# A hybrid decoder layer on one core: the prologue's input second in the queue, two modulation products in high and low halves, and two projection tiles begun between them

## What is computed

```python
def mixer_layer(x, c, ...):
    mod = jax.nn.silu(c) @ w_ada + b_ada          # 1024 -> 3072
    shift, scale, gate = jnp.split(mod, 3, axis=-1)
    h = rms_norm(x, pre_norm_w) * (1.0 + scale[:, None]) + shift[:, None]
    proj = h @ w_in                               # 1024 -> 3080, then pooling and gated delta rule
    ...
    y = jnp.concatenate([y_a, y_b], axis=-1) @ w_out
    x = x + gate[:, None] * rms_norm(y, post_norm_w)
```

## Time and profile before

| | before |
|---|---|
| median of 3 runs | 1133.2 us (1130.15 to 1133.69) |
| the profiled execution | 1131.2 us, its span 1129.4 us |
| TensorE busy | 1097.0 us, 97% |
| VectorE, ScalarE, GpSimd busy | 654.2, 358.0, 225.2 us |

### The profile page before, as it was taken

The page is one execution under the profiler, slowest core; times in us unless marked ns, Lnnn a source line. Parts: engine busy times, 40 slices in busy tenths (PEclk is TensorE's granted clock), DMA queues, the critical chain, the costliest instruction groups (busy, mean ns, idle before and its releaser), DMA issues.

```text
span 1129.4 us, 16484 instructions
## 1 busy us (share of the span) xinstructions
PE 1097.0 (97%) x6120; PEld 880.2 (78%) x6120; DVE 654.2 (58%) x1344; ACT 358.0 (32%) x713; POOL 225.2 (20%) x226
## 2 busy tenths in 40 slices
PE   7999999989999999999999999999999999999995
PEld 1578567877878888887878888887878888888774
DVE  1579884656345784555266883654346863454634
ACT  2365331234524511133324511224325420111201
POOL 1333443553400011231000002230000010522000
PEclk9999998999999999999999999999999999999998
DMA  9597555433756553224555552225673342322354
GB/s 367 199 321 269 207 199 194 151 129 132 269 209 244 200 187 123 102 76 156 219 205 205 192 191 100 108 80 186 224 275 114 148 149 76 113 75 75 110 203 164
DMA packets 44963, 196.09 MB, mean 174 GB/s; under 512 B 8858, under 2 KB 9626, under 8 KB 27348
## 3 DMA queue, kind: packets, MB, share of 16 engines
q1 hardware_dynamic: 44884, 195.03, 47.3%
HBM read 150.20 MB, written 44.81 MB: 173 GB/s over the span
## 4 chain that ended last, share of the span: by engine, by line
PE 68%; DVE 1%; issue 1%; POOL 0%; DVEq 0%; ACT 0%; POOLq 0%
PE acc L1991 12%; PE acc L1993 11%; PE acc L1992 11%; PE ring L2033 11%; PE acc L2020 2%; PE ring L2020 2%; PE ring L2022 2%; PE ring L2021 2%; PE acc L2022 2%; PE acc L2021 2%; PE ring L2178 2%; PE ring L2040 1%; PE ring L2049 1%; PE ring L2050 1%; PE ring L2209 1%
## 5 line engine op out<-in xcount | busy, mean ns | idle before, releaser
L1991 PE MATMUL acc<-hhi,wsl 128*128 128x512 f32 x768 | 315.8, 411 | 1.1 <-DVE y L1300 1.1
L1993 PE MATMUL acc<-hhi,wsl 128*128 128x512 f32 x768 | 301.2, 392 | 0.0
L1992 PE MATMUL acc<-hlo,wsl 128*128 128x512 f32 x768 | 300.4, 391 | 0.0
L1991 PEld LDWEIGHTS acc<-hhi,wsl 128*128 128x128 f32 x768 | 145.2, 189 | 32.7 <-issue 5.1
L1993 PEld LDWEIGHTS acc<-hhi,wsl 128*128 128x128 f32 x768 | 144.7, 188 | 32.0
L1992 PEld LDWEIGHTS acc<-hlo,wsl 128*128 128x128 f32 x768 | 145.3, 189 | 27.0 <-issue 1.4
L1187 DVE SCALAR_TENSOR_TENSOR cacc<-raw,cw,cacc 128x512 f32<-128x512 f32 x144 | 113.7, 789 | 5.1
L1777 POOL TENSOR_TENSOR wsl<-wraw,wsl 128x512 fp32r<-128x512 f32 x64 | 87.8, 1389 | 141.1 <-ACT wsl L871 141.1
L900 ACT ACTIVATE raw<-acc 128x512 f32<-128x512 f32 x48 | 28.6, 597 | 161.6 <-PE acc L1993 161.5
L1095 DVE TENSOR_TENSOR hlo<-htmp,hhi 128x512 fp32r<-128x512 f32 x32 | 22.1, 692 | 62.2 <-ACT hhi L845 61.9
L2020 PE MATMUL acc<-wsl,yhi 128*128 128x512 f32 x128 | 53.0, 414 | 1.8 <-DVE y L1300 1.6
(11 more groups left out here) (298 smaller groups left out, 1873.0 us busy)
## 6 DMA issues: line engine op xcount, KB each, us to landing
wsl<-kept_w SPq DMA_DIRECT2D x96, 1024.0 KB, 4.8
kept_w<-wsl SPq DMA_DIRECT2D x32, 1024.0 KB, 6.2
wraw<-in_w SPq DMA_DIRECT2D x64, 256.0 KB, 3.5
wada<-in_w_ada SPq DMA_DIRECT2D x8, 1024.0 KB, 13.0
xb<-in_x SPq DMA_DIRECT2D x16, 512.0 KB, 6.3
xres<-in_x SPq DMA_DIRECT2D x16, 512.0 KB, 5.7
out_y<-ytok SPq DMA_DIRECT2D x16, 512.0 KB, 8.2
wada<-in_w_ada SPq DMA_DIRECT2D x16, 256.0 KB, 4.8
```

What stands on the lines that cost most here:

```text
L1991: nc.tensor.matmul(acc[t % 2][:], w[:, 0, k], hi[:, k], start=(k == 0), stop=False)
L1992: nc.tensor.matmul(acc[t % 2][:], w[:, 0, k], lo[:, k], start=False, stop=False)
L1993: last = nc.tensor.matmul(acc[t % 2][:], w[:, 1, k], hi[:, k], start=False, stop=(k == KT - 1))
```

## The change

SyncE's queue now has the input directly after product 0 and the small tables, then product 1, the sample rows, the three raw halves, product 2, product 3.

Products 2 and 3 are no longer float32 matmuls. ScalarE copies each half of `wada[j]` (128 x 2048) to `wadh` in float32r, VectorE subtracts in place to `wadl`; `cin2` holds the high and the low half of the 9 rows side by side, 18 in all. `modulate_halves` runs two one-pass matmuls per k-step, with high and low weights, into a bank of `spare`. The turned result of 18 rows is folded to 9 columns by a matmul with `fold`. Products 0 and 1 remain.

The prologue's `h` is made as in the later blocks (`front_h`): ScalarE writes `htmp` and, in a second activation, `hhi`; VectorE only subtracts. ScalarE takes three raw halves ahead of the first `h` and the fourth behind the cuts.

```diff
+            def modulation_hi(j, e):
+                ks = slice(e * KT // 2, (e + 1) * KT // 2)
+                act.wait_ge(ada_in[j][e], 16)
+                nc.scalar.activation(wadh[j - 2][:, ks], wada[j][:, ks], ACT.Copy).then_inc(s_whi, 1)
+
+            for n in range(3):
+                half_hi(n)
+            act.wait_ge(s_half, 3)
+            front_h(act, PROLOGUE, 0)
+            front_h(act, PROLOGUE, 1)
+            modulation_hi(2, 0)
+            front_h(act, PROLOGUE, 2)
+            front_h(act, PROLOGUE, 3)
+            modulation_hi(2, 1)
+            modulation_hi(3, 0)
+            modulation_hi(3, 1)
+            half_hi(3)
+            act.wait_ge(s_half, 6)
+            for m in range(4, 8):
+                front_h(act, PROLOGUE, m)
...
+            def modulation_lo(j, e):
+                ks = slice(e * KT // 2, (e + 1) * KT // 2)
+                dve.wait_ge(s_whi, 2 * (j - 2) + e + 1)
+                nc.vector.tensor_tensor(wadl[j - 2][:, ks], wada[j][:, ks], wadh[j - 2][:, ks].bitcast(F32), ALU.subtract
+                                        ).then_inc(s_wlo, 1)
...
+            def modulate_halves(j, e):
+                pe.wait_ge(s_wlo, 2 * (j - 2) + e + 1)
+                if j == 2 and e == 0:
+                    pe.wait_ge(s_cin2, 3)
+                if j == 3 and e == 0:
+                    pe.wait_ge(s_half, 2)
+                rows = spare[4 - 2 * (j - 1)][0:2 + 2 * NS, :]
+                for k in range(e * KT // 2, (e + 1) * KT // 2):
+                    nc.tensor.matmul(rows, cin2[:, k], wadh[j - 2][:, k], start=(k == 0), stop=False)
+                    last = nc.tensor.matmul(rows, cin2[:, k], wadl[j - 2][:, k], start=False, stop=(k == KT - 1))
+                if e:
+                    last.then_inc(s_mod, 1)
...
             def first_tiles():
-                for t in range(2):
-                    for k in range(4):
-                        tile(0, t, k)
-                front_pe(pe, PROLOGUE, 7)
-                for t in range(2):
-                    for k in range(4, KT):
-                        tile(0, t, k)
+                for k in range(2):
+                    tile(0, 0, k)
+                    tile(0, 1, k)
+                front_pe(pe, PROLOGUE, 3)
+                modulate_halves(2, 0)
+                for k in range(2, 4):
+                    tile(0, 0, k)
+                    tile(0, 1, k)
+                modulate_halves(2, 1)
+                modulate_halves(3, 0)
+                front_pe(pe, PROLOGUE, 4)
+                front_pe(pe, PROLOGUE, 5)
+                front_pe(pe, PROLOGUE, 6)
+                turn_rows(2)
+                modulate_halves(3, 1)
+                turn_rows(3)
+                for k in range(4, KT):
+                    tile(0, 0, k)
+                    tile(0, 1, k)
+                    if k == 4:
+                        front_pe(pe, PROLOGUE, 7)
```

More of the change, by code:

```diff
@@ L682, in _ @@
                 sp.dma_start(xb[:, i], a["x"][0][:, i]).then_inc(x_in.sem, 16)
-            modulation(2)
+            modulation(1)
             sp.dma_start(xrow, a["xs"]).then_inc(sm_x0, 16)
@@ L723, in _ @@
                 raw_half(n)
+            modulation(2)
             modulation(3)
@@ L1131, in _ @@
                                                op0=ALU.add, op1=ALU.mult).then_inc(s_half, 1)
[L1132 to L1137 removed]
+            row_copy(0)
+            front_xn(dve, PROLOGUE)
+            row_copy(1)
+            dve.wait_ge(s_prm, 32)
+            modulation_columns(0)
+            front_lo(dve, PROLOGUE, 0)
+            front_lo(dve, PROLOGUE, 1)
+            modulation_lo(2, 0)
+            front_lo(dve, PROLOGUE, 2)
+            front_lo(dve, PROLOGUE, 3)
+            modulation_lo(2, 1)
+            modulation_lo(3, 0)
+            row_copy(2)
+            modulation_lo(3, 1)
+            row_copy(3)
+            modulation_columns(1)
+            for m in range(4, 8):
+                front_lo(dve, PROLOGUE, m)
             dve.wait_ge(*done("pool", "rx"))
@@ L1922, in turn_rows @@
                 for i in range(4):
-                    last = nc.tensor.transpose(spare[j // 2][:, 36 * (j % 2) + 9 * i:36 * (j % 2) + 9 * (i + 1)],
-                                               rows9[j][:, i * P:(i + 1) * P], ident[0:1 + NS, 0:1 + NS])
+                    col = 36 * (j % 2) + 9 * i
+                    to, part = spare[j // 2][:, col:col + 9], rows9[j][:, i * P:(i + 1) * P]
+                    if j < 2:
+                        last = nc.tensor.transpose(to, part, ident[0:1 + NS, 0:1 + NS])
+                    else:
+                        last = nc.tensor.matmul(to, part, fold[:], start=True, stop=True)
                 last.then_inc(s_tr, 1)
```

81 lines of the change are left out of this document (30 added, 51 removed).

## The result

| | kernel before | changed kernel |
|---|---|---|
| median of the runs | 1132.6 us (4 runs) | 1144.6 us (4 runs, 1142.1 to 1145.6) |
| ratio to before | | 1.0107 [1.0086, 1.0128] |
| profiled execution, time (span) | 1131.2 (1129.4) | 1142.1 (1140.3) |
| landmark: end of the two first tiles | 55.0 | 64.9 |
| small gate matmuls start | 60.7 | 73.5 |

The change costs 12.0 us by the medians and 10.9 by the two spans. I forecast slower, by 5, with 1141 as the upper end: the sign held, the size did not.

A forecast was written before the change was run, and what follows sets the result against it. TensorE, busy 97%, was taken as the bound, so only the prologue's end counted: +9.1 us to the second factors, −4.1 to the landmark, +5.0 in sum. Forecast 1137.2 us, range 1132.5 to 1141.

The forecast's parts named there:

- Steps 1 and 2: Input loading and product 1: squares from 14.4 us, 5.0 earlier; TensorE waits for weights to 16.9, finishes at 24.1.
- Step 3: VectorE's normalising: held by GpSimd's subtractions, three in a row adding 1.25 us; input ready at 27.4 us, before 31.2.
- rival A: Normalising on VectorE: GpSimd does not hold it, input ready at 23.7 us, only +1.6 us, 1133.8; chance 0.15.
- Steps 4 and 5: Chain to the modulation factors: first at 30.4 us, second at 51.6 (42.5 before), paced by ScalarE's cuts and VectorE's subtractions.
- First factors: Modulation columns' first half, after transposes and row turns: ready at 30.4 us, against 31.6 before.
- Second factors: Modulation columns' second half, after cuts, subtractions and quarter products: ready at 51.6 us, 9.1 later than before.
- Step 6: Second factors to the landmark: 8.4 us against 12.5 before, landmark at 60.0.
- Rival B: TensorE drops to its lower clock in the prologue's new gaps: +7 us, 1139.2; chance 0.13.
- gap of 1.54 us: TensorE's wait in before, filled by transposes behind it: read as losing nothing to the lower clock.
- late next: SyncE's queue behind the last input transposes: near 56 us, 6.5 later; raw halves still covered, else 1 us or so.

The follow-up runs named there:

- x6: Changed kernel with GpSimd's first three subtractions held until VectorE has normalised all four input pieces: 1140.2 us, ratio 1.0083.
- x4: Changed kernel with its queue and TensorE order, but products 2 and 3 in float32 as before, without cuts: 1150.4 us, ratio 1.0160.
- x1: Changed kernel plus three filler matmuls in each of three long TensorE waits in the prologue: 1144.8 us, ratio 1.0118.
- x9: Kernel before plus four dummy VectorE additions ahead of the gates' row copy, first pass only, lengthening one TensorE wait: 1136.4 us, ratio 1.0032.
- x13: Kernel before with x9's dummy additions and 18 filler matmuls in the wait they lengthen: 1132.3 us, ratio 1.0004.
- x2: Changed kernel with x1's fillers and 14 more behind the gate projection: 1143.3 us, ratio 1.0092.
- x18: Changed kernel with x1's fillers, VectorE's gates copy ahead of the first convolution, and 3 fillers behind the gates' matmuls: 1136.1 us, ratio 1.0047.
- x14: Kernel before plus five filler matmuls in its 1.2 us wait ahead of the gates' small matmuls, first pass only: 1130.5 us, ratio 0.9980.
- x15: x10 with VectorE's gates copy ahead of the first convolution, first pass only, and 3 fillers instead of 14 behind the gates' matmuls: 1129.0 us, ratio 0.9976.
- x10: Changed kernel with its prologue reordered (early cuts, GpSimd's subtractions behind the normalising), plus 4 and 14 fillers in two long waits: 1131.0 us, ratio 0.9989.
- x12: Changed kernel with before's input queue order, product 1 ahead of the input and product 2 behind it: 1151.8 us, ratio 1.0162.
- x3: Kernel before with only the loads in the new order; TensorE's order and float32 products stay: 1134.0 us, ratio 1.0017.
- x16: Kernel before with VectorE's gates copy ahead of the first convolution, first pass only: 1130.9 us, ratio 0.9988.

## Why the prediction was wrong, step by step

**Steps 1 and 2** held nearly: squares from 15.15 us (14.4), product 1 waits to 17.65 and ends at 24.7 (24.1). The input came 0.7 us later than I read from the megabytes ahead of it.

**Step 3** held: four normalising instructions in 6.70 us, ready at 28.1 (27.4), and x6 showed that it is GpSimd's hold, as step 3 had it against rival A. The Trainium skill ("SBUF — State Buffer", "Who interferes with whom") has whichever engine comes first hold the shared ports for a whole instruction, while the other is blocked. The trace agrees that VectorE is blocked, and goes beyond it in length: the 3.96 us here cover three instructions of GpSimd back to back.

**Steps 4 and 5**, the prices: cuts 1.9 and subtractions 2.25 us were right (1.92, and 4.49 for two); the last subtraction, beside GpSimd's, took 2.78. First factors 31.0 (30.4). Second factors 54.9 (51.6). The terms that I sized wrongly are two. The *turns with the fold* I had at 0.41 each, as before's turns; they are not transposes but float32 matmuls against a matrix, and take 1.05, so 2 × 0.64 = 1.3 us more (in x4, which turns with transposes, the second one takes 0.41). And the third group of transposes came 2.3 us late, 1.7 of it the clock (x1: 36.0), so ScalarE waited.

**Step 6**: second factors to landmark 10.0 us (8.4). In x1, at full clock, it is 8.45. This step was right but for the clock.

**Rival B** is what happened, and I gave it 0.13. I priced it at 2 us above the forecast. The profile shows 3.2 at the landmark (64.9 against 61.7), and then a third stretch that I did not name, of a further 1.6 us. The mistake was in the reading of before: I took its gap of 1.54 us without harm as the rule for gaps twice as long, and its first 169 us without a half-clock stretch as a property of the kernel rather than of a TensorE that was hardly ever without matmuls. And I wrote that every wait behind the prologue was about a microsecond. The view of TensorE's waits in before has one of 4.6 us, for VectorE (us in total, times, longest):

```profile
PE ring L2033 <- DVE wb L1610: 4.6, 1, 4.6
```

It ends at 252.1 us. The granted clock is 1.00 at 248 to 250 us, 0.89 at 250 to 252, 0.50 from 252 to 258 and 0.90 at 258 to 260: 6.8 us at half clock, begun in the wait. The price of a long wait stood in before's own trace. I had counted four waits of 2.5 to 3.3 us myself; x9 and x13 now show what one such wait brings. The rule of the Trainium skill that I cited there ("TensorE: Matmul & The Clock Gate", part 4, PE-mode transpose: transposes do not count as work for the gate) pointed the right way, but no run here parts transposes from plain waiting, so it is neither shown nor refuted.

**"So the change is worth exactly the microseconds by which it moves the end of the prologue"** was the failed assumption, and no rival had it growing: everything behind the landmark was to move as a block. Behind it the late second half let GpSimd's subtractions fall on VectorE's operations, and the gates' copy, third in that row, came 2.0 us later (+6.8 to +8.75 in x2). x18 moves the copy and the 2 us are gone. In the changed kernel's own profile this stretch lost 2.9 us, the three slowed operations on 512 columns included. Of what I listed as late next, SyncE's queue waited 27.8 us where before's waited 9.0, to 60.9 (I had 56); the tiles' weights showed no wait of TensorE.

The sum as it now stands, in the terms of the prediction: 5.0 forecast, + 0.6 first factors, + 1.3 turns (together +6.8 measured), + 2.0 gates' copy (8.75), + about 3 for the clock = 12. The last is the rest of the medians (12.0 − 8.75 = 3.3), not measured by itself, and not a sum over stretches (x2's total, with all four waits filled, is still 10.4 us above before by its ratio, 6.7 to 14.2). How many such stretches there are differs from run to run (mean clock 0.982 to 0.989 in the four of the changed kernel). The one near 170 us, behind waits that the change does not touch, is in the profiles of before, x14 and x15 and not in those of the changed kernel, x10 and x13. What decides that is open.

The halves were not the loss (x4), nor the queue (x12). The loss comes with the new order on the engines: its chain, cut after cut, leaves TensorE without work in a stretch where it had been nearly full. It is paid once by the chain's length and again at half clock.

## What to carry to other kernels

An edit that takes work off a full TensorE and makes it wait for a chain on two other engines is priced by that chain's length first, and then again by the lower clock that its waits can bring (here they were 2 to 5 us long). Look for such a wait in the kernel before: its trace has the price. Waits that can't be removed can be filled with matmuls of no use; here that was worth 3 to 4 us of 1136 for one wait of 4.7, and 2 us even in the kernel that nobody had touched. In the changed kernel itself, three or four filled waits alone did not lower the total by an amount that could be told. Ask at the end of the moved stretch which engine pairs now overlap that did not, and whether a small copy that TensorE waits for stands behind a long one that it does not need: moving it was worth 2 us in the changed kernel. And two edits that belong together can have opposite signs apart: the queue order cost up to 4 us alone (1.9 measured) and gained 6 to 7 with the rest.

## What I had not expected of the hardware

- Filling one wait (1.2 us, at 59.5 us) lowered the clock's share over the whole run by 1.9 us (x14). The profiles differ more than 100 us later: at 170 us before's has 6.8 us at half clock, x14's 3.4 and x13's none. Each is one execution, and why a filler at 60 us should matter there is open.
- The stretch at half clock that begins in a wait or behind it is not of one length: 3.4 us with the waits of 3.0 and 2.9 us in the changed kernel, 6.8 with 2.26 us in x3, 10.2 with 4.7 us in x9, 20.5 with 10 us in x12. Nor does it need a long wait: x16's profile has 3.4 us at half clock from 62.4 us, 2 us behind a wait of 0.93.
- Two VectorE operations on 64 columns took 1.28 and 1.19 us beside GpSimd's subtractions, and 0.26 and 0.20 without. They end at 67.15 and 68.37 us. If the three subtractions from 64.53 are equally long (1.26 each, an estimate), the second ends at 67.05 and the third at 68.31, so each operation seems to wait for the subtraction under way.
